# Squared-relu products: activation sums behind all evictions and weight sums, and a bank-by-bank wait for the second product

## The reference, cut to what matters

```python
def _sqrelu_mlp(x, w_up, w_down):          # w_up 1024 x 4096, w_down 4096 x 1024
    return jnp.square(jax.nn.relu(x @ w_up)) @ w_down
```

## Time and profile before

| | us |
|---|---|
| median of 3 runs | 2553.93 |
| range of the runs | 2552.10 to 2554.57 |
| the profiled execution, its own time | 2555.99 |
| span of the profiled execution | 2553.7 |
| granted PE clock, mean | 0.99 |

### The profile page before, as it was taken

The page is one execution under the profiler, slowest core; times in us unless marked ns, Lnnn a source line. Parts: engine busy times, 40 slices in busy tenths (PEclk is TensorE's granted clock), DMA queues, the critical chain, the costliest instruction groups (busy, mean ns, idle before and its releaser), DMA issues.

```text
span 2553.7 us, 32177 instructions
## 1 busy us (share of the span) xinstructions
PE 2484.0 (97%) x11945; PEld 2045.5 (80%) x11945; DVE 1513.2 (59%) x2037; ACT 949.5 (37%) x1288; POOL 1309.8 (51%) x957
## 2 busy tenths in 40 slices
PE   9999999999999999999999999999999999999998
PEld 8778777778888777778887888888888888888886
DVE  6667676687677567669224466666332243466666
ACT  4544333334565333334323433332332323433332
POOL 4225566555333656655333366665434433466664
PEclk9999999999999999999999999999999999999999
DMA  6113232223212223223222223332322222222232
GB/s 185 56 50 104 83 99 82 82 99 100 83 51 94 88 82 99 82 82 101 82 83 67 83 99 99 101 108 88 124 83 83 83 83 83 91 99 99 99 102 80
DMA packets 173704, 230.94 MB, mean 90 GB/s; under 512 B 11670, under 2 KB 128540, under 8 KB 173468
## 3 DMA queue, kind: packets, MB, share of 16 engines
q1 hardware_dynamic: 173596, 229.44, 27.4%
HBM read 227.32 MB, written 2.10 MB: 90 GB/s over the span
## 4 chain that ended last, share of the span: by engine, by line
PE 56%; issue 22%; POOL 14%; DVE 7%; ACT 1%; DMA 0%; POOLq 0%; DVEq 0%; SPq 0%; ACTq 0%
POOL w_lo L746 13%; PE banks L822 10%; PE banks L823 10%; PE banks L824 10%; PE banks L1611 4%; PE banks L1613 4%; PE banks L1612 4%; DVE work L2909 2%; PE banks L833 1%; PE banks L834 1%; PE banks L835 1%; DVE x_residual L2937 1%; DVE act_lo L2901 1%; PE banks L1103 1%; PE banks L1124 1%
## 5 line engine op out<-in xcount | busy, mean ns | idle before, releaser
L746 POOL TENSOR_TENSOR w_lo<-w_raw,w_hi 128x512 fp32r<-128x512 f32 (+1 forms) x820 | 1143.8, 1426 | 1224.0 <-ACT w_hi L1892 1214.0
L822 PE MATMUL banks<-h_hi,w_hi 128*128 128x512 f32 x1448 | 574.0, 396 | 0.9 <-POOL w_lo L746 0.9
L823 PE MATMUL banks<-h_lo,w_hi 128*128 128x512 f32 x1448 | 567.9, 392 | 0.0
L824 PE MATMUL banks<-h_hi,w_lo 128*128 128x512 f32 x1448 | 567.5, 392 | 0.0
L1892 ACT ACTIVATE w_hi<-w_raw 128x2048 fp32r<-128x2048 f32 x204 | 390.5, 1914 | 474.9 <-PE banks L1613 126.3
L822 PEld LDWEIGHTS banks<-h_hi,w_hi 128*128 128x128 f32 x1448 | 276.1, 191 | 64.9 <-issue 4.2
L823 PEld LDWEIGHTS banks<-h_lo,w_hi 128*128 128x128 f32 x1448 | 276.0, 191 | 58.6 <-issue 1.2
L824 PEld LDWEIGHTS banks<-h_hi,w_lo 128*128 128x128 f32 x1448 | 274.5, 190 | 58.4
L765 POOL TENSOR_TENSOR split_lo<-tokbuf,split_hi 128x512 fp32r<-128x512 f32 x132 | 166.8, 1293 | 0.0
L1611 PE MATMUL banks<-split_hi,act_hi 128*128 128x512 f32 x264 | 108.4, 410 | 47.3 <-DVE x_residual L2937 47.3
L3000 DVE TENSOR_TENSOR work<-banks,work 128x512 f32<-128x512 f32 x44 | 30.4, 692 | 199.4 <-PE banks L824 199.4
(11 more groups left out here) (329 smaller groups left out, 4773.0 us busy)
## 6 DMA issues: line engine op xcount, KB each, us to landing
w_raw<-in_ffn_w_in SPq DMA_DIRECT2D x44, 1024.0 KB, 5.1
w_raw<-in_ffn_w_up SPq DMA_DIRECT2D x32, 1024.0 KB, 5.3
w_raw<-in_ffn_w_down SPq DMA_DIRECT2D x52, 512.0 KB, 4.2
w_raw<-in_ret_w_in SPq DMA_DIRECT2D x24, 1024.0 KB, 5.1
w_raw<-in_ffn_w_out SPq DMA_DIRECT2D x36, 512.0 KB, 4.4
w_raw<-in_diff_w_qkv SPq DMA_DIRECT2D x12, 1024.0 KB, 5.1
w_raw<-in_fox_w_in SPq DMA_DIRECT2D x12, 1024.0 KB, 5.2
w_raw<-in_ret_w_out SPq DMA_DIRECT2D x8, 1024.0 KB, 5.0
```

The source lines that it names most:

```text
L746: nc.gpsimd.tensor_tensor(m.w_lo[:, sl, at], m.w_raw[:, sl, at], m.w_hi[:, sl, at].bitcast(F32), ALU.subtract)\
L822: mm(out, hi, x[0][:, k, :], start=k == 0, stop=False)
L823: mm(out, hi, x[1][:, k, :], start=False, stop=False)
L824: last = mm(out, lo, x[0][:, k, :], start=False, stop=k == kc - 1)
```

## The change

In the DVE list of a step all five evictions now come before the activation sums: evictions 2, 3 and 4 follow `corners_low` directly, then come `weight_mixes`, the three `mix` operations and `mixes_low`. In the last step the two `low` operations move behind eviction 4. On PE, product 1 (banks 0 and 1, which the up block filled before) no longer waits for both squares at once: its first three matmuls wait for the square of bank 0, its last three for that of bank 1. No instruction that computes is added or removed.

```diff
-def pe_product(m, operands, bank, begin=True, end=True):
+def pe_product(m, operands, bank, begin=True, end=True, second=None):
     for tile in range(2):
+        if tile and second:
+            second()
@@ pe_relu_products
+    def read(more):
+        pe.wait_ge(*m.upto(f"{t}_squared", along(i, [2 * g + more for g in gs])))
         elif n == 1:
-            pe.wait_ge(*m.upto(f"{t}_squared", along(i, [2 * g + 4 for g in gs])))
+            read(3)
-        pe_product(m, operands[product], RELU_BANKS[n], not resident or gs[0] == 1, not resident or gs[-1] == NR)
+        pe_product(m, operands[product], RELU_BANKS[n], not resident or gs[0] == 1, not resident or gs[-1] == NR,
+                   (lambda: read(4)) if n == 1 else None)
@@ dve_relu_mlp, step
         if more:
-            corners_low(after_it, i), mix(after_it, 0, i), mix(after_it, 1, i)
-        else:
+            corners_low(after_it, i)
+        evict(gs, 2, i), evict(gs, 3, i)
+        evict(gs, 4, i)
+        if not more:
             low(NR + 1, 0), low(NR + 1, 1)
-        evict(gs, 2, i), evict(gs, 3, i)
         if more:
-            mix(after_it, 2, i)
-        evict(gs, 4, i)
-        if more:
-            weight_mixes(after_it, i), mixes_low(after_it, i)
+            weight_mixes(after_it, i)
+            for part in range(3):
+                mix(after_it, part, i)
+            mixes_low(after_it, i)
```

## The result

| | before | after |
|---|---|---|
| median, us | 2553.01 | 2507.03 |
| range of the runs, us | 2550.41 to 2554.57 | 2506.35 to 2507.62 |
| the profiled execution, its own time, us | 2555.99 | 2506.46 |
| its span, us | 2553.7 | 2504.2 |
| granted PE clock, mean | 0.99 | 0.998 |

The ratio is 0.9821 with a 95% interval of 0.9804 to 0.9838: 46 us faster. The forecast was 2538, 15 us faster. The direction was right, the size three times too small, and the time lies 1 us above the lower edge of the range (2506), 2 us from the first rival's 2509. The two profiled executions differ by 49.5 us (2555.99 − 2506.46), and this is the sum that the profile has to explain.

A forecast was written before the change was run, and what follows sets the result against it. PE, 97% busy, was bounded by its pace, product 6's stall on eviction 2 and clock falls. Six pairs of 46.6 us gain 8.7 us a layer, less 1.1: two layers 15 us, giving 2540.5 profiled, 2538 median; range 2506 to 2552.

The forecast's parts named there:

- the first rival: Up-block stalls settle at 1.55 us in each step instead of alternating, clock stays up: 2509 us; chance 0.32.
- The stall at product 6: PE's wait for DVE's eviction 2 goes, removing about 2.3 us plus 0.11 for the restart.
- The wait for the second square: At product 1: 0.21 us plus 0.11 restart, some 0.3 us a step, taken as wholly gone.
- The chain to the up weights: DVE sums and mixes, ACT's splits, POOL's three tasks: up weights ready at N+23.4, PE wanting them at N+20.4.
- N: The moment at which PE could start the next up block.
- if a step was not held (s = 0), the next one is held by 3.0 us: At the up block: weights at N+23.4 against PE's N+20.4, so a 3.0 us stall follows an unheld step.
- The first term of the pair, 4.0 us: Up-block stall once in two steps: 3.0 us plus 0.97 us that the first weight sum costs POOL.
- the fall of the clock in each pair: PE's lower clock after each 4.0 us stall, taken as sure: 1.7 us of the pair's 46.6.
- the forecast's pattern: Steps alternate between no up-block stall and 4.0 us with a clock fall: 46.6 us a pair, before 47.75.
- The tail: Behind each layer's last step, low operations delay the folds from N+1.5 to about N+2.7: 1.1 us lost.
- Slower: Rival: POOL meets the three mixes as today, stall 6.2 us, a pair 48.8: 2565 us; chance 0.08.
- no gain: Rival: lower clock lasts longer after the stall, or product 6 waits as before: 2549 to 2559 us; chance 0.12.

The follow-up runs named there:

- the swap on ACT: The changed kernel with the high part of the activation sums made behind that of the down weights on ACT instead of ahead: 2490.0 us, ratio 0.9757.
- order only: The changed kernel without the bank-by-bank wait, product 1 waiting for both squares at once as before: 2516.9 us, ratio 0.9870.
- The kernel with a chain 1.2 us longer: The changed kernel with the two large mixes of each step made twice, behind the weight sums: 2559.6 us, ratio 1.0024.
- The push experiment: The changed kernel with two more mixes behind the weight sums in the first of the 13 steps alone: 2517.0 us, ratio 0.9868.
- the last experiment: Changed order, high parts swapped on ACT, quarter-by-quarter up-block wait (2471 us), plus the last step's two low parts ahead of evictions 2 to 4: 2467.4 us.

## Why the prediction was wrong

**What bounded the kernel before** was right in the place, and mis-sized in the clock's share. The falls of the clock were in the rows and priced at 1.68 us; seven in each layer make 23.5 us, and the summed distances show 22.5. (From product 6 to product 6 a layer has twelve stretches, not thirteen; seven of them at 0.93 is right.) But I treated them as something that any long stall brings, before as after, and so kept six of the seven falls of each layer in the sum for the kernel after.

**The stall at product 6** went, as said. **The wait for the second square** was taken as 0.3 us a step. That is its direct price; what it does to the stall at product 6 and to the clock is worth over 40 us when it stands alone. Why so much is shown only in its parts: shorter stalls, no fall of the clock, and the small gaps gone. I had costed it inside the new order only, never by itself.

**The chain to the up weights** was right: forecast N+23.4, measured 278.27 − 255.02 = 23.25 in the first step (POOL's end against N). The moved mixes take 0.69 us, as forecast, and POOL is slowed by 0.44 to 0.46 us for each DVE operation with two SBUF inputs. The move of the stall to the up block holds as well, and so does, in the changed kernel, that two steps take the chain plus 20.4 us: the steps of 22.0 us twice over, less 20.4, give a chain of 23.6 us. That half of a change in the chain's length shows in a step held for the shorter chain (the swap on ACT, 2490 against 2487) and not for the longer one, where DVE and POOL collided.

**The step that failed is "if a step was not held (s = 0), the next one is held by 3.0 us".** The first stall was not 0 but 0.35 us, for PE came to the up block 1.5 us earlier than I had it (255.02 against 256.54), while POOL's quarters came only 1.1 us earlier (255.13 against 256.2). So the second stall was 2.35 and not 3.0. This is where forecast and kernel part, for the weight sums are ready at N+1.43. With a stall of 3.0 POOL has two quarters left then, DVE gets in between them, and stall and chain both grow; with 2.35 the last quarter has just begun. POOL's and DVE's timelines of the kernel after:

```profile
273.28 4.99 POOL L746 TENSOR_TENSOR w_lo<-w_raw,w_hi 128x512 fp32r<-128x512 f32 x4
```

```profile
277.34 2.01 DVE L2881 TENSOR_TENSOR tokbuf<-w_raw 128x1024 f32<-128x1024 f32 x1
```

POOL began its last quarter at about 277.02, 0.3 us before DVE asked. DVE waited, POOL lost nothing (4.99 us), and the next stalls shrank to 1.2 and 1.4. By this working the point between the two is a stall of 1.43 + 1.25 = 2.68 us. That is an estimate; no run was made for it. What the traces have is a stall of 2.53 us without the collision (order only) and stalls of 4.1 us with it. The first term of the pair, 4.0 us, was for that reason wrong, and with it **the fall of the clock in each pair**: after the stall of 2.33 us nothing fell. A pair took 44.1 us (264.62 / 6) and not 46.6. Of these 2.5 us the clock is 1.7 and the stalls are 0.8, and the twelve pairs of both layers make 30 of the 34 us that the forecast missed. The kernel with a chain 1.2 us longer shows the forecast's pattern, at 47.55 us for two steps; the 46.6 forecast and half of the 1.2 would be 47.2.

**The first rival** was this case, with its working: 12 steps in 264.6 us, measured 264.62, and 2509 against 2507. I gave it 0.32, with two reasons against it: that the first stall is 0, and that the clock's fall resets the chain. The push experiment shows that even from a stall of 4 us the kernel comes back, in two steps where the clock stayed up behind the stall of 2.33 us and in four where it fell once more. **The range's lower end** lay only 3 us below this rival's own value, and the median lies just inside it. **The tail** of 1.1 us a layer was not there: between the last up block and the next layer's first transposes PE needs 32.2 us after and 32.6 before. The additions did begin later, at N+2.5 (2.7 forecast, N+1.5 before), but PE itself was held 0.9 us at that up block, and the two additions that take 3.47 us before take 2.70. The tail does show where nothing else hides it, as 1.0 us a layer in the last experiment. **Slower** and **no gain** did not come; but 1.2 us more of DVE work in each step brought no gain (2559.6), and with six more mixes in each step the kernel was slower than before (2612.8).

## What to carry to other kernels

When a stall is handed from one engine to another inside a loop, work out the first two or three passes with the start conditions as they are, to tenths of a microsecond, and then ask at which value an overlap tips: here 1.2 us more of chain turned 22.0 us a step into 23.8. Ask also whether the kernel comes back from a push: a single stall of 4 us did not keep it in the long pattern. Price each edit by itself as well as inside the whole, since two edits that both cure the same stall don't add. And where some passes run at the lower clock, count what their removal is worth as a term of its own: here it was nearly half of the gain. Waiting for a slow producer piece by piece instead of for all its pieces, and putting first on a queue what another engine waits for, together took the last stalls of the steps away here.

## What the runs showed of the hardware

The clock does not follow from the length of one stall alone. In the steps of the kept traces no gap under 2.2 us from matmul to matmul brought a fall. In the kernel before, the clock fell behind 14 of 24 stalls: behind all ten with a gap of 2.51 to 2.54 us, and behind 4 of the 14 with one of 2.20 to 2.26. Yet in the changed kernel gaps of 2.71 and 2.74 us left it up, as two of 2.92 us did in the kernel with the new order alone; in the kernel with the push a gap of 2.73 us brought a fall, two steps behind the fall before, and gaps of 2.71 and 2.72 did not. Behind gaps of 4.4 us and more it fell each time (12 of 12 in the kernel with two more mixes, 2 of 2 after the push).

Whether the small gap at product 1 weighs together with the stall stays open. For it: the kernel with the new order alone, which has the small gap (0.44 or 0.52 us), had a mean clock down to 0.994 in some executions, and the changed kernel, without it, never under 0.998. Against it: the gaps of 2.92 us had a small gap of 0.44 us some 8.5 us ahead and brought no fall, and in the step of rows 4 it was 0.44 us that stood ahead of a fall and, one step on, 0.52 us ahead of none. The stalls of the two kernels differ as well, and no run changed the distance between small gap and stall alone.

```profile
276.60 0.39 PE L1615 MATMUL banks<-split_hi,act_lo 128*128 128x512 f32 x1
281.04 0.79 PE L822 MATMUL banks<-h_hi,w_hi 128*128 128x512 f32 x1 [4.06 <-POOL w_lo L746]
281.63 0.63 PE L823 MATMUL banks<-h_lo,w_hi 128*128 128x512 f32 x1
```

These rows are from PE's timeline in the kernel with the push: after 4.06 us without work the first matmuls come at 0.6 us and then 0.43 us distance. On the shared access to SBUF the Trainium skill ("SBUF — State Buffer", section "Who interferes with whom") has it that the order of issue decides who blocks. That agrees: a weight sum that came 0.3 us after the start of a quarter waited for its end (2.01 us instead of 1.22), and one that found a gap between two quarters cost POOL 0.93 us.
